# Widening two helper tensors so that later SBUF tensors begin at multiples of 64 bytes

## The reference

```
block 1 (2 layers; tokens x and context ctx, 256 each, through one set of weights)
  mod = silu(c) @ ada_w + ada_b                       # shift, scale, gate per layer
  h   = rms_norm(x, g) * (1 + scale) + shift
  layer 0: q, k, v = h @ even_w_in   (window and neighbourhood attention, 512 tokens)
  layer 1: q, k, v = h @ odd_w_in    (differential attention, q and out for 256 tokens)
  x += gate * (attn @ w_out)
  x += gate * (relu(h @ w1) ** 2 @ w2)                # 1024 -> 4096 -> 1024
block 2 (2 layers; 256 tokens)
  p = h @ w_in  (latent, dilated and top-k attention), y = concat(...) * silu(gate)
  x = layer_norm(alpha * x + (1 + gate) * (y @ w_out))
```

## The kernel before

| tensor | address before | by 64 | by 128 |
|---|---|---|---|
| whi, wlo | 49280, 65664 | 0 | 0 |
| cst | 100544 | 0 | 64 |
| mhalf (4 bytes) | 113152 | 0 | 0 |
| MO, RC | 113184, 115232 | 32 | 32 |
| Hh, Hl | 117280, 133664 | 32 | 32 |
| aring, SB, AC, AR | 150048 to 178848 | 32 | 32 |
| pick (16 bytes) | 179872 | 32 | 32 |
| scs, stp | 179904, 180928 | 0 | 64 |
| Q0, Q1, HIDh | 181120 | 0 | 0 |
| HIDl, K0, V0, K1, V1 | 189312 to 205696 | 0 | 0 |
| Gh, Gl | 117280, 125472 | 32 | 32 |
| the other tensors of block 2, CQh and CQl among them | 133664 to 209056 | 32 | 32 or 96 |

## Time and profile before

### The profile page before, as it was taken

The page is one execution under the profiler, slowest core; times in us unless marked ns, Lnnn a source line. Parts: engine busy times, 40 slices in busy tenths (PEclk is TensorE's granted clock), DMA queues, the critical chain, the costliest instruction groups (busy, mean ns, idle before and its releaser), DMA issues.

```text
span 1352.6 us, 25050 instructions
## 1 busy us (share of the span) xinstructions
PE 1321.1 (98%) x9434; PEld 1168.0 (86%) x9434; DVE 990.8 (73%) x1734; ACT 668.6 (49%) x1358; POOL 193.9 (14%) x268
## 2 busy tenths in 40 slices
PE   7999999999999999999999999999999999999997
PEld 6786779888888888898996899999999988999967
DVE  6698778999887878978429565655665886865874
ACT  4427744631613315344238564566465566455573
POOL 0101213000000000123105600000210016020043
PEclk8999999999999999999999999999999999999999
DMA  8783134466885868834220345655475433455511
GB/s 309 274 239 120 49 110 141 156 218 216 311 309 205 286 212 292 298 112 151 94 94 1 108 146 167 205 183 171 140 267 178 140 128 104 157 167 168 170 49 47
DMA packets 67665, 233.15 MB, mean 172 GB/s; under 512 B 7280, under 2 KB 12400, under 8 KB 67312
## 3 DMA queue, kind: packets, MB, share of 16 engines
q1 hardware_dynamic: 67568, 231.84, 50.4%
HBM read 230.76 MB, written 1.05 MB: 171 GB/s over the span
## 4 chain that ended last, share of the span: by engine, by line
PE 87%; DVE 5%; ACT 2%; issue 2%; POOL 1%; DMA 1%; SPq 0%; ACTq 0%; DVEq 0%; POOLq 0%
PE ps L1710 25%; PE ps L1711 24%; PE ps L1712 24%; PE ps L1935 4%; PE ps L1964 3%; PE ps L1995 2%; DVE wlo L957 1%; DMA aring<-aall 1%; PE ps L1979 1%; DVE ps L1031 1%; ACT wk L719 1%; PE ps L1727 1%; ACT whi L599 1%; DVE ps L1233 1%; DVE small L1246 0%
## 5 line engine op out<-in xcount | busy, mean ns | idle before, releaser
L957 DVE TENSOR_TENSOR wlo<-raw,whi 128x1024 fp32r<-128x1024 f32 (+1 forms) x284 | 347.7, 1225 | 151.4 <-ACT whi L599 145.7
L599 ACT ACTIVATE whi<-raw 128x1024 fp32r<-128x1024 f32 (+1 forms) x284 | 296.4, 1044 | 267.7 <-PE ps L1712 267.1
L1710 PE MATMUL ps<-Hh,whi 128*128 128x256 f32 (+1 forms) x896 | 303.4, 339 | 3.0 <-DVE wlo L957 1.0
L1711 PE MATMUL ps<-Hl,whi 128*128 128x256 f32 (+1 forms) x896 | 300.0, 335 | 0.0
L1712 PE MATMUL ps<-Hh,wlo 128*128 128x256 f32 (+1 forms) x896 | 300.0, 335 | 0.0
L1710 PEld LDWEIGHTS ps<-Hh,whi 128*128 128x128 f32 x896 | 169.2, 189 | 25.5 <-issue 5.2
L1712 PEld LDWEIGHTS ps<-Hh,wlo 128*128 128x128 f32 x896 | 169.1, 189 | 19.1
L1711 PEld LDWEIGHTS ps<-Hl,whi 128*128 128x128 f32 x896 | 169.4, 189 | 18.3
L1710 PE MATMUL ps<-Gh,whi 128*128 128x256 f32 x624 | 176.2, 282 | 0.5 <-DVE Gl L1164 0.4
L1710 PE MATMUL ps<-HIDh,whi 128*128 128x256 f32 (+1 forms) x536 | 176.5, 329 | 0.0
L1711 PE MATMUL ps<-HIDl,whi 128*128 128x256 f32 (+1 forms) x536 | 176.3, 329 | 0.0
(11 more groups left out here) (266 smaller groups left out, 2062.9 us busy)
## 6 DMA issues: line engine op xcount, KB each, us to landing
raw<-wall SPq DMA_DIRECT2D x270, 512.0 KB, 4.0
aring<-aall SPq DMA_DIRECT2D x144, 512.0 KB, 4.6
raw<-wall SPq DMA_DIRECT2D x14, 384.0 KB, 3.1
AL<-ali SPq DMA_DIRECT2D x14, 192.0 KB, 5.3
X<-xin SPq DMA_DIRECT2D x2, 1024.0 KB, 6.6
BI<-rpb SPq DMA_DIRECT2D x4, 512.0 KB, 9.7
out<-X SPq DMA_DIRECT2D x4, 256.0 KB, 2.4
cst<-const SPq DMA_DIRECT2D x1, 960.0 KB, 8.3
```

The costliest lines, as they stand in the source:

```text
L599: act.activation(whi[:, slot, 0:n], raw[:, slot, 0:n], ACT.Copy).then_inc(sem("w_hi"), 1)
L957: dve.tensor_tensor(wlo[:, slot, 0:n], raw[:, slot, 0:n], whi[:, slot, 0:n].bitcast(F32), ALU.subtract)\
L1710: pe.matmul(o, a[0], b[0], start=first, stop=False)
L1711: pe.matmul(o, a[0], b[1], start=False, stop=False)
```

## The change

`mhalf` grows from 1 to 16 floats per partition and `pick` from 4 to 16, of which the name `pick` still means the first 4. No instruction is added, removed or moved.

```
-        mhalf = sb("mhalf", [P, 1])
+        mhalf = sb("mhalf", [P, 16])
...
-        pick = sb("pick", [P, 4], F32, b1)
+        pick = sb("pick", [P, 16], F32, b1)[:, 0:4]
```

## The result

The changed kernel takes 1346.45 us (median of four runs, 1344.96 to 1348.33) against 1355.53 us of the kernel before beside it: a ratio of 0.9937 with a 95% interval of 0.9926 to 0.9949, 9.1 us less. The forecast was 3.2 us less; the time lies on the low bound of the range (1346.5), and the sign was right.

The account below looks back on a forecast made before the run. TensorE, busy for 1321.1 of 1352.6 us, was taken to bound the kernel through mm3's matmuls. The terms -9.1 + 5.9 = -3.2 us took the median 1356.1 to 1352.9 us, range 1346.5 to 1357.3.

Parts of the forecast that it names:

- The measured paces: Matmul starts in the trace before: aligned moving operands 7.5 ns faster at 512 columns, 1.7 ns slower at 256.
- The pace follows the remainder by 64 of the moving operand: Float32r matmuls: the moving operand's start modulo 64 bytes sets the pace; the stationary operand does not seem to matter.
- Term 1: 512-column matmuls with H moving: 1217 steady ones, each 7.5 ns faster, 9.1 us less.
- Term 2: 256-column matmuls with H, G or CQ moving: 3485 steady ones, each 1.7 ns slower, 5.9 us more.
- Term 3: Matmuls with HID or weights moving: they keep their remainder by 64 and so their pace, 0.
- The steps of nought: Parts put at 0, among them attention's plain float32 matmuls (-0.5 to +0.5 us), elementwise writes, transfers and mhalf's memset.
- step 6: Transfers: aring might land earlier and shorten TensorE's one wait; gain between 0 and 1.6 us, taken as 0.
- The 3.5 us between span and median: The runs' median lay 3.5 us above the profiled span, so the forecast was set against the median, 1356.1 us.
- Only the 512-column term: Rival: 256-column paces stay near 118 ns, leaving only -9.1 us: 1347.0 us; chance 0.14.
- The coarser grid: Rival: hardware wants 128-byte starts, H, G and CQ keep their pace, HID takes it on: +3.7 us, 1359.8 us; chance 0.14.
- VectorE eats it: Rival: VectorE's work does not fit the shorter w1 stretch in the first MLP; result near 0, counted with no change.
- No change: Rival: H's and HID's paces differ through place or writing instructions, not remainder: 1356.1 us; chance 0.14.

Follow-up runs that it names:

- block2_only: Kernel before with 32 unused bytes at the start of block 2's scope and no other edit: 1348.69 us, ratio 0.9956.
- d64_64_192: Kernel before with unused bytes putting H and HID at distance 64 from the weights modulo 256, G at 192: 1340.13 us, ratio 0.9888.
- the repeat: Kernel before and changed kernel, each run and profiled once more without edit: 1354.91 and 1345.10 us.
- shift32: Kernel before with an unused 32-byte tensor ahead of X, so all tensors move and all distances stay: 1354.47 us, ratio 0.9995.
- grid128: Kernel before with mhalf widened to 32 floats and pick to 16, so H, G, CQ and HID begin at multiples of 128 bytes: 1355.25 us, ratio 0.9997.
- d224: Kernel before with unused bytes putting H, HID and G all at distance 224 modulo 256: 1355.45 us, ratio 1.0005.
- wlo128: Kernel before with wlo moved 128 bytes against whi, and H, HID and G at distance 0 from whi: 1353.96 us, ratio 0.9988.

## Why the prediction was right in sign and wrong in its terms

*TensorE's pace goes straight into the span.* Right. In block2_only and d64_64_192 the sums over paces, -5.3 and -15 us, came back as -5.9 and -14.5.

*The measured paces.* Right as readings: the 7.5 ns at 512 columns came back in the repeat, the 1.7 ns at 256 as 2.0.

*The pace follows the remainder by 64 of the moving operand.* This is the step that failed, and terms 1 to 3 of the sum stood on it. Before the change remainder and distance cannot be told apart: `H` and `G` had 32 and distance 160, `HID` had 0 and distance 0. shift32 separates them, and it is the distance. My check that "stationary operands do not seem to matter" took weights over `H` at 120.0 ns for the aligned pace; it was the pace of distance 96, which at 256 columns happens to be the same as that of 0.

- Term 1, `H` at 512 columns: forecast -9.1 us, measured -1.1. From distance 160 to 192 there is little to win; 64 gives 6.3 us and 0 gives 8.6.
- Term 2, `H`, `G` and `CQ` at 256 columns: forecast +5.9 us, measured -7.7. Distance 192 is the fastest of all there; how often its faster pace comes is partly chance.
- Term 3, `HID` and moving weights: forecast 0, measured +1.5 at 512 columns, -2.4 for `HID` and -1.6 for the weights at 256.

The terms' errors are 8.0, -13.6 and -2.5 us, so they cancelled in part, and the right sign was luck: with only term 1 as measured, the same sum would have been 4.8 us slower. The steps of nought held. VectorE's busy time went from 990.8 to 988.9 us; the matmuls of lines 1935, 1964 and 1995 took 144.85 us from start to start before and 144.87 after (together 9% of the chain by the earlier trace rows, not under 9%). The one wait that step 6 bounded from the good side only, at 0 to 1.6 us of gain, went the other way, from 1.6 and 1.8 us to 2.7 and 2.8; no run isolates it.

*The 3.5 us between span and median.* Misread, though the forecast does not hang on it. Every execution with both numbers on record lies 1.8 to 2.1 us above its own span, so only that much is time outside the first and last instruction; the rest of the 3.5 us is scatter, the profiled execution having been a fast one. The profiled execution of the changed kernel was the slowest of its four (1348.33 us, span 1346.4), which is why the spans differ by 6.2 us and the medians by 9.1.

*The rivals.* "Only the 512-column term" gave 1347.0 us and is nearest in time, by the wrong road: the 512 columns gained least. The coarser grid had two things right, `H` staying near its old pace at 512 columns (233.3) and `HID` getting slower (228.9, not 234), but it is refused by grid128: at multiples of 128 `HID` goes to 233.3 ns. "VectorE eats it" found no test, as `w1` hardly became shorter (44.79 us). "No change" is refused by the time; its thought, that `H` and `HID` differ in more than a remainder, was the better one, and d224 shows in what. The 16-byte lines of the Trainium skill, page "SBUF — State Buffer", section "Specifications (TRN2)", do not foresee these paces: all distances in the table are multiples of 32 and so of 16, and lie up to 7.5 ns apart. The same page of the Trainium skill, in the section "A bandwidth-pool intuition that's wrong (but worth ruling out)", gives the loads of stationary operands a second, independent read port. The runs here do not agree with an independence of timing: moving one operand against the other by 32 bytes changed the pace, from 226.7 to 233.3 ns for `HID` at distance 0 and 32. Whether that happens at a port they do not show.

## What to carry to other kernels

Where a stream of float32r matmuls, each with its own load, sets the time, look at the address of the moving operand less that of the stationary one modulo 256, and measure two or three distances by unused bytes ahead of one of them: here it was worth 14.5 us of 1355 and up to 7.3 us the other way. The best distance depends on the width (0 or 64 for 512 columns, 192 for 256). Only steps of 32 bytes, this type and these two widths were measured. Before an alignment is taken for a cause, move everything by the same amount: that costs one run and separates a place from a distance.

## What was not expected of the hardware

- Moving weights changed pace from 120.0 to 117.8 ns when only the stationary operand was moved by 32 bytes.
- Many paces lie above the streaming time by whole pieces. At distance 0, 512 columns take 106.7 ns more than 256 (226.7 less 120.0), which is one column for each cycle at 2.4 GHz, the clock granted here (1.00). By that 512 columns stream in 213.3 ns and 256 in 106.7. The three matmuls of a product at 512 columns then take 40.0 ns more than streaming at distance 0, 46.7 at 64, 53.3 in wlo128 and 60.0 at 32, 96, 128, 192 and 224: the time of 96, 112, 128 and 144 columns. At 256 columns the paces 113.3, 117.8 and 120.0 are 48, 80 and 96 columns more for three. All are multiples of 16. Distance 160 does not fit (234.2 is 150 more for three), and why it goes by sixteens is not shown.
- At distance 192 with 256 columns there are two paces, 113.4 and 117.8 ns, and the stream keeps one for a whole stage: in the changed kernel `G` had 117.8 in the stage from 971 us on and 113.4 in that from 1059 on. It is not that distance alone: `HID` at distance 64 had 113.3 in its first stage of 256 columns and 117.8 in the others. What puts a stage on one or the other was not tried.
- Alignment as such was worth nothing measurable: 0.9995 (0.9985 to 1.0005) for all tensors moved by 32 bytes, 0.9997 for all later ones at multiples of 128.
